# Two matmuls of 256 columns in place of one of 512 in the split-precision products of a transformer kernel

## The reference

```
for l in range(2):
    a_x, a_c = modulate(rms_norm(h_x)), modulate(rms_norm(h_c))
    y_x, y_c = mixer(a_x, a_c, w_in[l], ...)      # y_c only for l = 0
    h_x += gt1 * y_x;  h_x += gt2 * conv_ffn(modulate(rms_norm(h_x)), w_up[l], w_down[l])
    if l == 0: the same two steps for h_c
```

## Time and profile before

| | us |
|---|---|
| three timed runs | 2643.65, 2647.99, 2648.91 (median 2647.99) |
| the profiled execution, its own time | 2645.86 |
| its span, first to last instruction | 2644.1 |
| first layer (two joints and the mixer, up to the end of its feed-forward net) | about 60 to 1020 of the span |
| second layer, mixer | about 1020 to 1265 |

### The profile page before, as it was taken

How to read it: one execution, slowest core, us unless ns; L and a number is a source line. 1 busy time by engine, 2 the same in 40 slices (tenths; PEclk the granted TensorE clock), 3 DMA queues, 4 the chain that set the end, 5 groups by cost and what they waited for, 6 DMA issues and landing times.

```text
span 2644.1 us, 42166 instructions
## 1 busy us (share of the span) xinstructions
PE 2526.0 (96%) x17790; PEld 2235.6 (85%) x17790; DVE 1564.6 (59%) x2692; ACT 1224.7 (46%) x2026; POOL 188.9 (7%) x234
## 2 busy tenths in 40 slices
PE   6999999999999998989999999999999999988999
PEld 3876777787677777878899999998899999976999
DVE  3244345346556565454668877667666766766665
ACT  4234434335233234363565564455544544465543
POOL 0000000010000001000010011000100100034200
PEclk9999999999999999999999999999999999999999
DMA  7234522223355443233445546543365456431553
GB/s 257 77 102 161 167 84 76 88 83 117 120 169 166 135 152 118 90 112 102 138 155 195 185 161 208 183 160 128 128 203 181 159 194 207 163 112 33 191 191 129
DMA packets 337389, 382.13 MB, mean 145 GB/s; under 512 B 7409, under 2 KB 301297, under 8 KB 337201
## 3 DMA queue, kind: packets, MB, share of 16 engines
q1 hardware_dynamic: 334656, 370.37, 42.7%
q0 software_dynamic: 2544, 9.06, 1.1%
HBM read 378.36 MB, written 1.05 MB: 143 GB/s over the span
## 4 chain that ended last, share of the span: by engine, by line
PE 82%; DVE 7%; ACT 7%; DMA 1%; issue 1%; POOL 1%; SPq 0%; POOLq 0%; ACTq 0%; DVEq 0%
PE PS L1332 22%; PE PS L1334 22%; PE PS L1333 22%; DVE WL L2040 2%; PE PS L1382 1%; ACT WH L1711 1%; PE PS L1369 1%; PE PS L1370 1%; PE PS L1371 1%; PE PS L1472 1%; DMA RAWB<-in_w_ada 1%; PE PS L1349 1%; PE PS L1447 1%; PE PS L1515 1%; PE PS L1482 1%
## 5 line engine op out<-in xcount | busy, mean ns | idle before, releaser
L2040 DVE TENSOR_TENSOR WL<-RAWB,WH 128x1024 fp32r<-128x1024 f32 (+2 forms) x613 | 736.5, 1209 | 540.1 <-ACT WH L1711 538.9
L1332 PE MATMUL PS<-AH,WH 128*128 128x256 f32 (+1 forms) x2912 | 908.9, 312 | 6.4 <-DVE WL L2040 6.4
L1334 PE MATMUL PS<-AH,WL 128*128 128x256 f32 (+1 forms) x2912 | 897.2, 308 | 0.0
L1333 PE MATMUL PS<-AL,WH 128*128 128x256 f32 (+1 forms) x2912 | 896.8, 308 | 0.0
L1711 ACT ACTIVATE WH<-RAWB 128x1024 fp32r<-128x1024 f32 (+2 forms) x613 | 625.3, 1034 | 290.0 <-PE PS L1334 169.6
L1332 PEld LDWEIGHTS PS<-AH,WH 128*128 128x128 f32 x2912 | 547.3, 188 | 60.5 <-issue 19.5
L1334 PEld LDWEIGHTS PS<-AH,WL 128*128 128x128 f32 x2912 | 547.3, 188 | 31.2
L1333 PEld LDWEIGHTS PS<-AL,WH 128*128 128x128 f32 x2912 | 547.7, 188 | 29.6 <-issue 0.5
L1332 PE MATMUL PS<-BH,WH 128*128 128x256 f32 (+1 forms) x1440 | 446.4, 310 | 0.8 <-DVE WL L2040 0.8
L1334 PE MATMUL PS<-BH,WL 128*128 128x256 f32 (+1 forms) x1440 | 439.3, 305 | 0.0
L1333 PE MATMUL PS<-BL,WH 128*128 128x256 f32 (+1 forms) x1440 | 439.2, 305 | 0.0
(11 more groups left out here) (312 smaller groups left out, 2707.3 us busy)
## 6 DMA issues: line engine op xcount, KB each, us to landing
RAWB<-in_f_in SPq DMA_DIRECT2D x88, 1024.0 KB, 5.1
RAWB<-in_w_in SPq DMA_DIRECT2D x52, 1024.0 KB, 5.0
RAWB<-in_w_ada SPq DMA_DIRECT2D x48, 1024.0 KB, 5.3
RAWB<-in_w_up SPq DMA_DIRECT2D x44, 1024.0 KB, 5.3
RAWB<-in_f_out SPq DMA_DIRECT2D x40, 1024.0 KB, 5.0
RAWB<-in_w_down SPq DMA_DIRECT2D x20, 1024.0 KB, 5.1
RAWB<-in_sb_qkv SPq DMA_DIRECT2D x12, 1024.0 KB, 5.1
RAWB<-in_w_out SPq DMA_DIRECT2D x8, 1024.0 KB, 5.1
```

The costliest lines, as they stand in the source:

```text
L1332: pe.matmul(out, h, xh[:, 0:T], start=k == 0, stop=False)
L1333: pe.matmul(out, h, xl[:, 0:T], start=False, stop=False)
L1334: i = pe.matmul(out, l, xh[:, 0:T], start=False, stop=k == g.kt - 1)
L2040: dve.tensor_tensor(c.part("WL", p), c.raw(p.slab)[:, k0:k1, c0:c1], c.part("WH", p).bitcast(F32), ALU.subtract).then_inc(up("lo", ("lo", ...
```

## The change

The three matmuls of a step of the contraction are each written as a loop over pieces of 256 columns. Where T is 256 nothing changes; where T is 512 each matmul becomes two, on the two halves of the same bank, each with a load of its own of the same stationary tile. Only the very first matmul of a tile carries the start flag, only the very last one the stop flag and the signal.

```
@@ -1329,9 +1329,12 @@
                 xh, xl = c.operand(g.src, k)
                 h, l = hi[:, k, s.c:s.c + 128], lo[:, k, s.c:s.c + 128]
                 on.wait_ge(*at(*g.ready(k)))
-                pe.matmul(out, h, xh[:, 0:T], start=k == 0, stop=False)
-                pe.matmul(out, h, xl[:, 0:T], start=False, stop=False)
-                i = pe.matmul(out, l, xh[:, 0:T], start=False, stop=k == g.kt - 1)
+                for a in range(0, T, 256):
+                    pe.matmul(out[:, a:a + 256], h, xh[:, a:a + 256], start=k == 0 and a == 0, stop=False)
+                for a in range(0, T, 256):
+                    pe.matmul(out[:, a:a + 256], h, xl[:, a:a + 256], start=False, stop=False)
+                for a in range(0, T, 256):
+                    i = pe.matmul(out[:, a:a + 256], l, xh[:, a:a + 256], start=False, stop=k == g.kt - 1 and a + 256 == T)
             i.then_inc(up("acc", ("acc", g.name, s.n), *([("wdone", s.p.p)] if s.x else [])), 1)
```

## The result

The changed kernel takes 2661.01 us, median of 8 runs (2655.24 to 2667.06), against 2647.27 us, median of 8 (2637.53 to 2653.44). The ratio is 1.0049, 95% interval 1.0032 to 1.0066, so it is slower by about 13 us (the two medians are 13.7 us apart). The forecast was +14.5 us. The profiled execution of after took 2655.24 us with a span of 2653.4 us, 9.3 us more than the profiled one of before.

A forecast was written before the change was run, and what follows sets the result against it. TensorE, 96% busy, was taken to bound the kernel. Split steps +17.5 us less 3.0 us taken back by waits gave +14.5 us on 2648.0: 2662.5 us, own range 2655 to 2670, 8 times in 10 2646 to 2676.

The forecast's parts named there:

- Removed and added: First-layer steps of 512 columns, 686.7 ns, become six matmuls of 256: 706.4 or 680.0 ns; over 1056 steps +20.8 or -7.1 us.
- Which end: Split first-layer products: 12 in 100 at 113.3 ns a matmul, the rest at 117.7 ns, giving +17.5 us.
- What lies beside other work: TensorE's waits, mostly in the mixers: 25 waits shrink by one tile's growth each, taking back 3 us (bounds nothing and 6).
- The entry: First matmul of a product after attention: some 100 ns above steady spacing in both forms, paid once per tile, nothing extra.
- the lower clock: Stretches at 1.2 GHz: two halves cost nothing extra, at most 0.3 us of the sum; the clock falls no more often.
- the bank: Successive matmuls no longer add to the same columns of the bank: costed at nothing.
- the instructions: 3168 more loads and matmuls, put at about 18% more for the first layer: costed at nothing.
- More than the common spacing: Rival for the split products: each half takes 120 ns, 11.1 ns more per cut, +35 us, 2680 us; chance 0.08.
- Closer spacing, faster: Rival at product entry: all six matmuls settle at 113.3 ns, 6.7 ns less a step, 2640.9 us; chance 0.12.
- Half the price: Rival: half the steps at each of two spacings, +6.9 us, less 1.4 in waits, 2653.5 us; chance 0.12.
- The exposed load: By the skill's rule 3168 further loads go unhidden at 188 ns each, +596 us, about 3244 us; chance 0.
- Back-to-back issue gap: Skill's warm matmul spacing of N/2.4 + 2.5 ns: a cut costs 2.5 ns, +7.9 us less what waits take back.

The follow-up runs named there:

- The quarters: The changed kernel, but each matmul of 512 columns is cut into four of 128, each with its own load, instead of two of 256: 3347.12 us.
- the uneven parts: The changed kernel, but each matmul of 512 columns is cut into 384 and 128 columns instead of 256 and 256: 2819.63 us.
- the inserted short matmuls: The kernel before, uncut, with a discarded matmul of 16 to 240 columns ahead of most tiles (540 insertions): 2703.49 us.
- the first experiment: The changed kernel with each step's six matmuls reordered, three on the left half, then three on the right: 2660.03 us, ratio 1.0040.
- the kernel at distance 0: The kernel before with weight buffers moved to 0 modulo 256 bytes from the activations: 2667.26 us; the changed kernel so placed: 2703.10 us.
- distance 64: Weight buffers moved to 64 bytes past a multiple of 256 from the activations: kernel before 2637.63 us, changed kernel 2628.97 us.

## Why the forecast held, and which of its steps did not

**Removed and added.** Right, and the heart of it. The price of a cut is the difference of spacings and nothing else, +19.7 ns or -6.7 ns a step; both ends appear in the trace of after with the values forecast, 117.8 and 113.3 ns. The extra load is hidden. The quarters, the uneven parts and the inserted short matmuls say how: a matmul with a load takes the longer of its columns and about 112 ns, and 256 columns are just above that. That the load sets the 112 ns is likely, by the 27 ns behind a short matmul, but no run has a stream of these matmuls without loads.

**Which end: the step that failed.** "I put 12 in 100 at the closer spacing"; it was 36. With the measured share the steps come to 0.64 x 20.8 - 0.36 x 7.1 = +10.8 us, where 17.5 were forecast. I had judged the new pattern by the second block, and the closer share there (6.0 in 100 before, 2.2 after) was no guide: by stage the share of split products runs from none to 60 in 100, and in the first experiment from none to all.

**What lies beside other work: failed too.** "These 25 waits, one tile each, take back 3 us": they took back 0.6 us between matched events outside the short stretch. Most of these waits do not shrink with the tile before them; those between 1025 and 1270 us, for instance, last the same 4.7, 2.5, 0.9 and 0.8 us in both kernels, line by line. The one wait that shrank, by 2.6 us, is for weights, and it is as short in some kernels without a split. With both corrections the steps give +10.2 us, near the +9.2 us of the five matched stretches and inside the interval of the medians (0.0032 to 0.0066 of 2647, 8.5 to 17.5 us). The two errors were 6.7 and 2.4 us of opposite sign. Both terms lie outside the forecast's own ranges (5 to 20 in 100, 1 to 6 us), so that it came within 2 us of the measured difference is in part luck. Some 3 us between +10.2 and the +13 of the runs are left. In the profiled pair the second block's mean distance is 0.17 ns longer in after, 1.6 us over some 9400 distances, but that mean moves from run to run. The clock is the other candidate, next.

**The entry, the lower clock, the bank, the instructions.** All four were put at next to nothing, and for three of them no cost showed. Neither the order of the halves nor with it the change of columns matters (first experiment). Issue gaps grew by 0.9 us at the largest group, though the prediction spread the added instructions too thin: 18% more is the figure for the whole program, and the feed-forward stretch alone went from 1556 to 2756 matmuls. The entry is as forecast: in that stretch the first matmul of a product starts on average 329 ns ahead of the second in before and 218 ns in after, 100 ns above the steady spacing both times. The lower clock is less clear. The profiled run of after has a mean clock of 0.992, but its eight runs average 0.9890 and the eight of the first experiment 0.9891, while 43 runs of before beside the experiments average 0.9904. Over those 43 a clock lower by 0.001 goes with 2.3 us more, so this would be some 3 us, as much as is left over. That the change makes the clock fall more often isn't shown by so few runs; the prediction had it as a sign of being wrong, and had no price for it.

**The rivals.** "More than the common spacing" fell for this placement, but its figure of 120 ns is exactly what the kernel at distance 0 has; the rival was real one placement away. "Closer spacing, faster" fell here, and happened in part at distance 64. "Half the price" (+6.9 us) was nearer to the truth in its share than the forecast was (50 and 12 around 36), which is why the range had to reach down to it.

**The exposed load.** Against the Trainium skill (TensorE: Matmul & The Clock Gate, "The mechanism": overlap only when the row group differs) the runs are plain: in the quarters a load with a record of about 191 ns and its matmul pass every 111 to 112 ns, all on the whole array. But the prediction took too little from that page of the Trainium skill: the same section also lets a load be pulled ahead when it goes to the background weight buffer, so that the page does not plainly forecast exposed loads for this change. Whether that buffer is what hides the loads here, no run shows. The same page of the Trainium skill, "LDWEIGHTS", puts a load at its columns / 1.2 ns, 107 ns for 128, in rough agreement with the floor of about 112 ns. The formula that the prediction took from the Trainium skill's "Back-to-back issue gap" is given there for a matmul by itself, not for a stream of loads and matmuls.

What stays open: why a distance of 64 or 192 allows two spacings, and what picks one when a product is entered. No run here separates moduli above 256, and none moved the activations or the result tiles, so distance and the weights' own address can't be told apart.

## What to carry to other kernels

Cutting a matmul and loading its tile again is nearly free only as long as each part has as much work as one load takes (here 256 columns against 112 ns); below that each part costs a full load. Price such an edit by the distances between starts of long undisturbed stretches, never by durations. If a trace shows two spacings for the same code, find what picks one before trusting the average of another stage. Before tuning the instructions, look at where the weights lie in memory: here that alone made the changed kernel 1.5% slower (1.0204 / 1.0049) or 1.3% faster (0.9916 / 1.0049), and turned the sign of the change in the feed-forward net.

## What the runs showed of the hardware that was not expected

- Where the weights lie modulo 256 bytes, with the activations fixed, moves the spacing of these 32-bit matmuls: 256 columns from 113.9 ns (distance 64) to 119.7 ns (0), 512 columns from 228.2 ns (0) to 234.1 ns (96). The best place for the one is not the best for the other.
- The change's price for each matmul of 512 by distance, from matched events in the feed-forward net: +11.7 ns at 0, +4.2 ns at 192, -1.9 ns at 64. By mean spacings over the first layer it is +3.2 ns at 192 and -2.7 ns at 64.
- Matmuls of 128 columns with a load each start 111 to 112 ns apart, hardly faster than 256 columns at the closer spacing (113.3 ns), and a further matmul of 16 to 240 columns adds about 110 ns whatever its width.
- TensorE holds one of two spacings for up to tens of us of the same code. A short matmul put between never brought the closer one (some 360 cases) and ended it each time it met it (three cases).
